# Two sums stages of a mixture-of-experts layer: every second late row is added by the matrix engine

## The reference

```python
def token_block(args):               # 128 tokens at a time
    hb, eb, gb = args                # activations, the 128 picked experts, their weights
    u = jnp.take(u_tab, eb, axis=0)
    act = jax.nn.gelu(jnp.einsum('tkd,td->tk', u, hb), approximate=False)
    vv = jnp.take(v_tab, eb, axis=0)
    return jnp.einsum('tk,tkd->td', gb * act, vv)
```

## Time and profile before

| | |
|---|---|
| median of 3 runs | 2760.39 us (2756.93 to 2764.67) |
| the profiled execution, its own time | 2758.64 us |
| its span, first to last instruction | 2756.7 us |
| busy in the span | PE 1868.5 us (68%), DVE 1880.9 (68%), POOL 1086.2 (39%), ACT 404.0 (15%) |
| rows that VectorE adds (line 2039) | 464, some 1.2 to 1.3 us each |
| rows that TensorE adds (line 881) | 40 (160 matmuls), in two stretches |

### The profile page before, as it was taken

How to read it: one execution, slowest core, us unless ns; L and a number is a source line. 1 busy time by engine, 2 the same in 40 slices (tenths; PEclk the granted TensorE clock), 3 DMA queues, 4 the chain that set the end, 5 groups by cost and what they waited for, 6 DMA issues and landing times.

```text
span 2756.7 us, 24246 instructions
## 1 busy us (share of the span) xinstructions
PE 1868.5 (68%) x8389; PEld 1349.1 (49%) x8389; DVE 1880.9 (68%) x3436; ACT 404.0 (15%) x904; POOL 1086.2 (39%) x1059
## 2 busy tenths in 40 slices
PE   7988444275555362644635647779628999999998
PEld 5786111265343161233333135564317887478873
DVE  2758998889578879988889997676795342153001
ACT  1321001122103020012111010000104100041000
POOL 2004435677255555755665765456460000000000
PEclk8999556596676685867767878899869999999999
DMA  9629999999899999989999989999983594433443
GB/s 341 229 78 373 399 398 399 342 380 371 319 393 405 399 401 400 361 324 405 403 398 388 358 311 394 394 391 403 330 321 109 182 304 161 145 109 93 152 152 122
DMA packets 357625, 850.47 MB, mean 309 GB/s; under 512 B 23832, under 2 KB 147072, under 8 KB 357376
## 3 DMA queue, kind: packets, MB, share of 16 engines
q0 software_dynamic: 148672, 538.17, 50.9%
q1 hardware_dynamic: 208832, 310.76, 32.2%
HBM read 847.79 MB, written 1.05 MB: 308 GB/s over the span
## 4 chain that ended last, share of the span: by engine, by line
PE 35%; DMA 23%; DVE 21%; issue 15%; POOL 4%; ACT 1%; SPq 1%; DVEq 0%; POOLq 0%; ACTq 0%
PE bank L1151 13%; PE bank L1170 8%; DMA RING<-in_peer_v,EX 7%; DMA RING<-in_peer_u,EX 5%; DMA W<-in_w_up 3%; DMA WORK<-in_peer_u,EX 3%; DVE ACC L2021 3%; POOL RING L1296 3%; DMA W<-in_w_gate 3%; PE bank L452 2%; DMA W<-in_ada_w 2%; PE bank L1095 2%; DVE ACC L2039 2%; DVE hrows L2039 2%; PE bank L440 1%
## 5 line engine op out<-in xcount | busy, mean ns | idle before, releaser
L1151 PE MATMUL bank<-HT,W 128*128 128x256 f32 x1984 | 460.9, 397 | 61.2 <-DMA W<-in_w_gate 30.0
L1296 POOL DMA_INDIRECT RING<-in_peer_v,EX x341 | 387.6, 1137 | 195.7 <-DVE hrows L2039 77.1
L1296 POOL DMA_INDIRECT RING<-in_peer_u,EX x343 | 326.5, 952 | 345.5 <-DVE ACC L2021 217.7
L2021 DVE SCALAR_TENSOR_TENSOR ACC<-RING,hrows 128x1024 bf16<-128x1024 f32 x343 | 406.9, 1218 | 81.2 <-DMA RING<-in_peer_u,EX 74.9
L1151 PEld LDWEIGHTS bank<-HT,W 128*128 128x128 f32 x1984 | 394.8, 200 | 126.8 <-DMA W<-in_w_up 33.3
L489 PE MATMUL bank<-W,CACT 128*32 128x512 f32 x544 | 117.0, 957 | 205.1 <-DMA W<-in_w_ada 119.7
L1296 POOL DMA_INDIRECT WORK<-in_peer_v,EX x171 | 194.5, 1138 | 107.4 <-DVE hrows L2039 51.9
L1296 POOL DMA_INDIRECT WORK<-in_peer_u,EX x169 | 160.4, 949 | 179.0 <-DVE ACC L2021 156.0
L1170 PE MATMUL bank<-W,WORK 128*128 128x512 f32 x528 | 227.3, 593 | 3.6 <-DVE WORK L2727 3.6
L2021 DVE SCALAR_TENSOR_TENSOR ACC<-WORK,hrows 128x1024 bf16<-128x1024 f32 x169 | 201.6, 1218 | 36.2 <-DMA WORK<-in_peer_u,EX 35.5
L2039 DVE SCALAR_TENSOR_TENSOR ACC<-RING,ACTS,ACC 128x1024 f32<-128x1024 f32 x155 | 198.5, 1281 | 27.5 <-DMA RING<-in_peer_v,EX 27.1
(11 more groups left out here) (433 smaller groups left out, 2847.0 us busy)
## 6 DMA issues: line engine op xcount, KB each, us to landing
W<-in_ada_w SPq DMA_DIRECT2D x36, 1024.0 KB, 11.8
W<-in_w_gate SPq DMA_DIRECT2D x33, 1024.0 KB, 7.8
W<-in_w_up SPq DMA_DIRECT2D x33, 1024.0 KB, 5.7
W<-in_w_down SPq DMA_DIRECT2D x33, 1024.0 KB, 5.0
W<-in_w_in SPq DMA_DIRECT2D x32, 1024.0 KB, 15.7
W<-in_w_ada SPq DMA_DIRECT2D x32, 1024.0 KB, 17.3
W<-in_peer_wq SPq DMA_DIRECT2D x24, 1024.0 KB, 18.1
W<-in_w_o SPq DMA_DIRECT2D x10, 1024.0 KB, 15.9
```

What stands on the lines that cost most here:

```text
L1151: mm = pe.matmul(bs[j][:, g * S:(g + 1) * S], w[:, k, j * P:(j + 1) * P], HT[:, k, :], start=(k == 0 and g == 0), stop=(k == DC - 1 and g ...
L1296: gp.indirect_dma_start(SLOT[g % NS], None, rows, bass.IndirectOffsetOnAxis(EX[:, t, k:k + 1], 0))\
L2021: ve.scalar_tensor_tensor(out=JUNK[:, g % 2, :], in0=SLOT[g % NS], scalar=1.0, in1=HB[:, :], op0=ALU.mult, op1=ALU.mult, accum_out=ACTS[:, ...
```

## The change

The two lists in `BY_PE` go in steps of two where they went in steps of three, from the same first picks: 78, 80, ... 124 (24 rows where there were 16) and 54, 56, ... 124 (36 where there were 24). VectorE's loop over the picks skips those that are in the list, so it does 8 and 12 rows fewer. ScalarE makes as many diagonals as there are rows. The place for them was 24 matrices wide; it becomes one place of 24 and one of 36 matrices that end at the same address, the larger reaching down over tables of attention that no later step of that tile reads. No other line is changed.

```diff
-        DIAG = carve(5124, 3072).rearrange("p (k n) -> p k n", k=24)
+        DIAG = [carve(8196 - 128 * n, 128 * n).rearrange("p (k n) -> p k n", k=n) for n in (24, 36)]
...
-        BY_PE = {(0, 1): [78 + 3 * i for i in range(16)], (1, 0): [54 + 3 * i for i in range(24)]}
+        BY_PE = {(0, 1): [78 + 2 * i for i in range(24)], (1, 0): [54 + 2 * i for i in range(36)]}
...
-                        mm = pe.matmul(bs[hf][:, :], DIAG[:, i, :], SLOT[g % NS][:, hf * 512:(hf + 1) * 512],
+                        mm = pe.matmul(bs[hf][:, :], DIAG[t][:, i, :], SLOT[g % NS][:, hf * 512:(hf + 1) * 512],
...
-                    ins = A(DIAG[:, i, :], ident, ACT.Copy, scale=ACTS[:, k:k + 1])
+                    ins = A(DIAG[t][:, i, :], ident, ACT.Copy, scale=ACTS[:, k:k + 1])
```

## The result

The changed kernel takes 2744.08 us (median of 8 runs, 2733.48 to 2753.89), the kernel before in the same rounds 2758.66 (8 runs, 2753.43 to 2764.67). The ratio is 0.9947, 95% interval 0.9933 to 0.9962: 14.6 us faster, between 10.5 and 18.5. The forecast was 12.9 us, to 2747.5. A second measurement beside other kernels (the last experiment) gave 0.9952, 0.9939 to 0.9965.

What follows compares the result with a forecast made beforehand. VectorE was taken to bound both shared stages until rows run short; 6.0 us (2.7 steps, 3.3 stock) and 6.9 us (3.6 and 3.3) sum to 12.9, so 2760.39 - 12.9 = 2747.5 us, range 2738 to 2758.

Steps and rivals of the forecast that it cites:

- The bound: Both shared stages: VectorE is the limit until the last row, as long as rows arrive fast enough.
- The stock: End of each shared stage: pick 127's row lands 3.3 us before VectorE starts it; using this up gains 3.3 us.
- The step: GpSimd's time per gather in the shared stages: falls from 1.484 and 1.475 to 1.42 us, gaining 2.7 and 3.6.
- long gathers: GpSimd in the shared stages: a gather starting while VectorE adds into ACC takes longer, 1.72 us for pick 121.
- Where VectorE waits: Line 2039, late in both shared stages: VectorE shows waits of a few us for DMA, where it had none.
- First rival, supply at its ceiling: Gathers in both shared stages: steps stay at 1.475 to 1.484 us, only 6.6 us gained, 2753.8; chance 0.14.
- VectorE the limit to the end: Both shared stages: rows are always there, so all removed VectorE rows count, 23.8 us gained, 2736.6; chance 0.09.
- TensorE behind: Both shared stages: TensorE's clock stays at 1.2 GHz, 3.75 us a row, 39 us slower, 2800; chance 0.07.
- the threshold of 2.84: TensorE in the shared stages: two gathers take 2.84 us; below that average per row nothing is lost.
- Given back: Dots stage after the shared stages: it waits earlier for transfers and returns the gain, 2760; chance 0.06.
- Diagonals and transfer of the gain at nothing: ScalarE's added diagonals cost nothing on the path; the stages' gain passes to what follows with nothing lost.

Runs made afterwards that it cites:

- the last experiment: The changed kernel itself measured again, beside two other kernels on the same chip: 13.2 us faster than the kernel before, ratio 0.9952.
- second stage alone: Kernel before with the new TensorE list only in the second shared stage, the first keeping its 16 picks: 9.1 us faster than the kernel before.
- the last version: Changed kernel with 44 second-stage picks on TensorE and VectorE's rows from pick 54 all into hrows (PSUM): median 2739.06 us, 19.3 faster than before.
- short rows: Changed kernel, but from pick 100 VectorE adds only 64 of 1024 columns of its rows in both shared stages: 24.3 us faster than the kernel before.
- more rows on TensorE: Changed kernel with 46 instead of 36 picks on TensorE in the second stage: 17.7 us faster than the kernel before.
- four half rows: Changed kernel with four half rows on TensorE for each pick instead of two: 23.2 us slower than the kernel before.
- diagonals alone: Kernel before with its old lists, but ScalarE writes 24 and 36 diagonals into the larger tables: 0.3 us faster (-3.6 to 3.0).

## Why the prediction was right, and where its sizes were off

- **The bound.** VectorE sets the end until rows run short: as forecast. The account closes from VectorE's side too: 9.5 us of rows removed less 2.0 of new waits is 7.5, and the first stage gave 7.0; 14.3 less 4.3 is 10.0, and the second gave 10.1.
- **The stock** (3.3 us a stage). Used up in the first stage: VectorE starts pick 127 at 1177.05, 4.5 us after its gather ended, and by the trace the row landed at 1177.0, 5.4 us after the gather's start. In the second it landed 5.5 us after 1587.72, at 1593.2, and is started at 1594.64: 1.4 us of stock are left (before 3.6). From the end of the gather to VectorE's start it is 8.5 us before, 1594.64 - 1588.86 = 5.8 now, 2.7 less.
- **The step** (1.42, 2.7 and 3.6 us) was the term mis-sized: 1.397 and 1.362, so 62.32 - 58.67 = 3.7 and 97.38 - 89.91 = 7.5. With 3.3 and 2.7 of stock that is 7.0 and 10.2, the stages' gain; in the first stage the close fit is partly luck, since there the row of pick 127 waits 4.0 us less after its gather and the gather of pick 85 comes 0.7 us later behind the first pick. The prediction let only waits for slots shrink and took the long gathers as given. In the second stage GpSimd's idle time fell by 2.6 us and its work by 4.9: with 12 rows fewer there are fewer adds into ACC for a gather to meet. 23 gathers started in one before and lost 9.3 us by it, 16 do now and lose 4.6; `route` cost 2.0 and costs 1.4. How much of it falls differs by run: with the second stage alone the work fell by 2.6 us and the idle time by 4.5. In the first stage the work fell by 1.2 and the idle time by 2.4.
- **Where VectorE waits.** Said to be late in both stretches; the waits stand in the middle (the longest before pick 99 in both stages), and none after pick 100, where VectorE and the gathers are level (steps of 1.42 and 1.35 us from there).
- **First rival, supply at its ceiling** (0.14). The steps did get shorter, and the stretches moved 368 and 384 GB/s, and 399 in the last version. The rule of the Trainium skill (SBUF — State Buffer, "A bandwidth-pool intuition that's wrong (but worth ruling out)") of about 358 GB/s to a core is not borne out: the measurement decides. The shortest steps that any version reached, at 391 to 399 GB/s, are 1.30 to 1.35 us, and those with short rows are GpSimd's own work.
- **VectorE the limit to the end** (0.09). Wrong by 23.8 - 17.1 = 6.7 us; short rows and more rows on TensorE both take work from VectorE and bring little of it in time.
- **TensorE behind** (0.07). The condition did not hold; its arithmetic did, with four half rows. The clock stayed high: TensorE stands idle 0.56 us before pick 120 instead of 1.84, and the granted clock rose from 0.82 to 0.97. This rise is not where the gain comes from: in the kernel before no gather of either stretch waited over 0.30 us for a slot of TensorE's. The prediction set an isolated pick's 1.98 against the threshold of 2.84; back to back a pick needs 1.72, so there is more room than it thought.
- **Given back** (0.06). Layer 1's last line 2068 comes 9.2 us earlier (2049.99, before 2059.17) in a run whose first stage began 7 us late.
- **Diagonals and transfer of the gain at nothing**: the first is shown by the run with the diagonals alone. For the second, the stages' change and the change in time agree within 3.5 us in all eleven kernels of the table with both stages measured, now one and now the other being larger (changed 17.1 and 14.6, short rows 23.0 and 24.3, four half rows 22.1 and 23.2 longer), so no steady loss shows on the way.

## What to carry to other kernels

When two engines feed one end, size a relief by the slower of what is taken from the one and what the other can still deliver, and look for side effects of the removed work on the supplier: here two thirds of what the second stage's gathers gained in the changed kernel, and over a third with that stage's list alone, was work that got shorter, with fewer adds running beside it. Take an engine's capacity from back-to-back work, not from the length of an isolated instruction. Compare stages from a common first event; the span of one profiled run hid most of this gain.

## What was not expected of the hardware

- A pair of half rows (128x512, f32) takes 1.98 us alone and 1.72 back to back, at the high clock.
- A gather that starts in an add whose two inputs are in SBUF ends 0.81 us after the add, so it takes up to 2.0 us instead of 0.94; with the accumulator in PSUM 1 of 42 and 1 of 66 were over 1.4 us. Doubling the adds into SBUF did not double the time lost.
- TensorE's granted clock in the stretches went from 0.82 to 0.97 with 1.5 times the picks.
